# Moving one conditioning piece of a fused two-block kernel from the SSD stage into the attention heads

## The reference, cut to what matters

```
for i in range(2):                                   # DEPTH = 2
    x = x + 0.5 * swiglu(rms_norm(x), ...)           # d_ff 2816
    proj = rms_norm(x) @ w_in[i]
    xbc = silu(causal_depthwise_conv(xbc)) ; y_ssd = ssd_mixer(xbc, dt_raw, z, ...)
    y_att = dilated_attention(q, k, v)               # 16 heads of 64
    x = x + concatenate([y_ssd, y_att]) @ w_out[i]
    x = x + 0.5 * swiglu(rms_norm(x), ...)
...
c_act = silu(c)
mod   = c_act @ w_ada + b_ada                        # 1024 -> 6 * 1024
modf  = c_act @ w_ada_f + b_ada_f                    # 1024 -> 2 * 1024
```

## Time and profile before

| quantity | value |
|---|---|
| median of 3 runs | 2202.26 us (2196.20 to 2210.37) |
| profiled execution, time | 2203.71 us |
| profiled execution, span of the core | 2201.9 us |
| mean granted TensorE clock | 0.978 of full |
| PE busy, share of the span | 96% |
| DVE busy | 75% |
| ACT busy | 50% |
| POOL busy | 21% |

### The profile page before, as it was taken

One profiled execution on the slowest core, in us unless ns is written; L12 is line 12 of the kernel. 1 busy time (PEld: TensorE's weight loads), 2 busy tenths in 40 slices (PEclk: granted clock), 3 DMA queues, 4 the chain that ended last, 5 costly groups with the idle time before them and its releaser, 6 DMA issues. The chain is left out here.

```text
span 2201.9 us, 34859 instructions
## 1 busy us (share of the span) xinstructions
PE 2115.3 (96%) x13433; PEld 1839.4 (84%) x13433; DVE 1655.9 (75%) x2247; ACT 1111.8 (50%) x1291; POOL 455.8 (21%) x239
## 2 busy tenths in 40 slices
PE   6999999999999999999999998999979999999996
PEld 6998999559998998999658997999957777777775
DVE  5665887548666765778538655788789999999998
ACT  4343353334433433354324343524348888888885
POOL 8600180809004500081718100000010000000000
PEclk9999999999998999999999999999989999999999
DMA  8854564436655655464336653435649999999994
GB/s 260 267 183 141 158 213 141 143 125 226 211 176 186 232 184 178 145 200 154 134 134 211 199 193 96 153 116 166 235 155 362 369 369 378 364 362 377 367 366 171
DMA packets 238996, 484.33 MB, mean 220 GB/s; under 512 B 10612, under 2 KB 178848, under 8 KB 222528
## 3 DMA queue, kind: packets, MB, share of 16 engines
q1 hardware_dynamic: 226880, 443.58, 57.5%
q0 software_dynamic: 11424, 37.44, 5.1%
q10 hardware_dynamic: 608, 2.14, 0.2%
HBM read 482.03 MB, written 1.09 MB: 219 GB/s over the span
## 5 line engine op out<-in xcount | busy, mean ns | idle before, releaser
L748 PE MATMUL misc<-xh,ring_low 128*128 128x256 f32 x1536 | 427.9, 279 | 0.0
L747 PE MATMUL misc<-xl,high_b 128*128 128x256 f32 x1408 | 394.0, 280 | 9.4 <-DVE xl L2117 6.9
L749 PE MATMUL misc<-xh,high_b 128*128 128x256 f32 x1408 | 392.0, 278 | 0.0
L748 PEld LDWEIGHTS misc<-xh,ring_low 128*128 128x128 f32 x1536 | 291.9, 190 | 3.4
L2779 DVE TENSOR_TENSOR ring_low<-ring,high_b 128x2048 fp32r<-128x2048 f32 x128 | 287.1, 2284 | 0.0
L747 PEld LDWEIGHTS misc<-xl,high_b 128*128 128x128 f32 x1408 | 267.2, 190 | 13.7 <-DVE xl L2117 7.1
L749 PEld LDWEIGHTS misc<-xh,high_b 128*128 128x128 f32 x1408 | 267.0, 190 | 0.0
L2126 DVE TENSOR_TENSOR ring_low<-ring,high_b 128x2048 fp32r<-128x2048 f32 x88 | 226.2, 2611 | 39.7 <-ACT high_b L1613 39.7
L1890 ACT ACTIVATE high_b<-ring 128x2048 fp32r<-128x2048 f32 x124 | 235.7, 1914 | 33.9 <-DMA ring<-in_w_dram 33.0
L1644 ACT ACTIVATE arena<-arena 128x256 f32<-128x256 f32 x88 | 36.8, 418 | 427.7 <-DVE arena L2160 427.7
L1310 PE MATMUL misc<-high_b,ue 128*128 128x512 f32 x512 | 204.2, 399 | 1.9 <-DVE ue L2822 1.2
(11 more groups left out here) (426 smaller groups left out, 4964.1 us busy)
## 6 DMA issues: line engine op xcount, KB each, us to landing
ring<-in_w_dram SPq DMA_DIRECT2D x128, 1024.0 KB, 7.8
ring<-in_w_in_dram SPq DMA_DIRECT2D x72, 1024.0 KB, 5.5
ring_d<-in_w_dram SPq DMA_DIRECT2D x128, 512.0 KB, 5.2
ring<-in_ffn_w_gate_dram SPq DMA_DIRECT2D x44, 1024.0 KB, 5.4
ring<-in_ffn_w_up_dram SPq DMA_DIRECT2D x44, 1024.0 KB, 7.8
ring_d<-in_ffn_w_down_dram SPq DMA_DIRECT2D x88, 512.0 KB, 7.3
arena<-in_w_ada_dram POOLq DMA_DIRECT2D x48, 512.0 KB, 4.4
ring<-in_w_out_dram SPq DMA_DIRECT2D x20, 1024.0 KB, 4.9
```

What stands on the lines that cost most here:

```text
L747: pe.matmul(dst, wh, ml, start=start, stop=False, **kw)
L748: pe.matmul(dst, wl, mh, start=False, stop=False, **kw)
L749: return pe.matmul(dst, wh, mh, start=False, stop=stop, **kw)
```

## The change

Pool's piece 4l+1 no longer waits for the convolutions of the SSD mixer (`conv_done`) but for the gated SSD rows (`ysd_ready`). PE takes it in the ninth step of the heads (h = 9), between the turned weights of head 7 and the values of head 6; DVE takes it at the end of its step 9. Its fill, M, moves into the list of the attention fills behind T of head 7.

```diff
@@ attention_fills
         if h in TURNS:
             order.append(("Y", TURNS[h]))
+        if h == MOD_AT:
+            order.append("M")
     order.append(("Y", 3))
+MOD_AT = 9
@@ fills
-                  (("v", l, 3), 1), (("qkt", l), 8), (("mod", 4 * l + 1), 1), (("yt", l), 4), (("att", l), 2 * HEADS + 4),
+                  (("v", l, 3), 1), (("qkt", l), 8), (("yt", l), 4), (("att", l), 2 * HEADS + 5),
@@
+    for l in range(DEPTH):
+        FILL.first["mod", 4 * l + 1] = FILL["att", l] + AF["M"]
@@ PE, before the turns of the SSD rows
-                modulation(4 * l + 1)
                 pe.wait_ge(ysd_ready, l + 1)
@@ PE, in the loop over the steps
                         turn_values(TURNS[h])
+                    if h == MOD_AT:
+                        modulation(4 * l + 1)
                     if h >= 3:
                         values(h - 3)
@@ Pool, first block of a piece
                         if p % 4 == 1:
-                            pool.wait_ge(conv_done, NX * (p // 4 + 1))
+                            pool.wait_ge(ysd_ready, p // 4 + 1)
```

## The result

| | before | after |
|---|---|---|
| median | 2202.15 us (8 runs, 2196.20 to 2210.37) | 2221.00 us (8 runs, 2217.04 to 2227.22) |
| ratio | | 1.0081 [1.0062, 1.0099] |
| profiled execution, time and span | 2203.71, 2201.9 us | 2222.78, 2221.0 us |
| mean granted clock | 0.978 | 0.973 |

The change costs 18.9 us, three times the forecast 5.9 and 2 us beyond the upper end of the range. Timed again on another chip, beside the repeats of experiments 3 to 5, it took 2220.36 us (10 runs), 1.0075 [1.0050, 1.0101]. The medians of the experiments and all ratios leave out three slow executions, of 2394 us (experiment 4), 5410 and 6033 us (kernel before).

The account below looks back on a forecast made before the run. PE, busy 96% of the span, was taken to set the time. The terms -3.3 - 0.2 + 3.8 + 0.6 + 1.8 + 1.0 + 2.2 = +5.9 us gave a forecast of 2208 us, range 2197 to 2219.

Parts of the forecast that it names:

- part 1: SSD stage without Pool: PE's gap near 300 us shrinks to 1.0 us; gain 3.3 us in layer 0, 0.2 in layer 1.
- part 2: Eight matmuls moved from ahead of the SSD rows to step 9: +3.8 us, and +0.6 for the clock after the longer standstill.
- Part 3: Bank order: at step 10 scores 11 wait about 0.9 us for line 2422 to free their bank; +1.8 us in all.
- Part 4: Pool beside steps 10 to 18 stretches line 2405, +1.0 us; at the attention's end, a split of line 2126, +2.2 us.
- rival 2: Heads, steps 10 and 11: the clock falls in both layers, +3.4 to +6.8 us, 2215 us at most; chance 0.2.
- One empty step and not two speaks against: Argument against the clock falling at steps 10 and 11: one step there lacks an output unit, not two.
- the spare time: Step 9, layer 0: piece 1 ready at about 439.0, PE asks at 442.2, 3.2 us to spare.
- rival 1: SSD stage: all DVE stretches were on the path, 2193 or 2188 us; milder form 2203; chance together 0.25, strong form 0.05.
- rival 3: Step 9 comes too early for piece 1, PE waits 7.6 us; 12.8 us a layer, 2234 us; chance 0.05.
- rival 4: Nothing moves: layer 0's gap has another reason and the heads hide the rest; 2202 us; chance 0.05.

Follow-up runs that it names:

- Experiment 3: Kernel after, one matmul of 8 columns in place of eight of 1 column for pieces 1 and 5: 2213.25 us, 1.0056; again 2214.13 us.
- experiment 4: Kernel after, the piece's eight columns in unused columns of the bank of scores 9, no fill of their own: 2216.49 us, 1.0069; again 2218.23 us.
- experiment 5: Kernel after, eight columns in scores 9's bank by one matmul: 2202.82, again 2207.93 us; its estimate for the unedited after: work and waiting +12, clock loss +9.
- experiment 2: Kernel after, Pool waits for `conv_done` again, PE and DVE still take the piece at step 9: 2215.72 us, 1.0056.
- experiment 1: Kernel before, Pool's sums and products for pieces 1 and 5 cut to one column, loads and waits kept: 2204.14 us, 1.0008.
- experiment 6: Kernel after, Pool's arithmetic for pieces 2 and 6 cut to one column: 2207.95 us, 1.0019.
- experiment 8: Nothing changed, a second profile of each kernel: before 2200.52 us, after 2202.63 us.
- Experiment 7: Kernel after, Pool's first two loads of pieces 3 and 7 issued only after PE took the piece before: 2220.78 us, 1.0083.

## Why the prediction was wrong

The direction was right, and the time stayed within 1%, which had 0.94 of the chance. The size was not: 13 us are missing from the sum. Of its terms +6.4 us were work and waits and -0.5 us clock (-1.1 in part 1, +0.6 in part 2). The estimate of experiment 5 has some 12 and some 9 us. So two steps of the prediction failed: it counted the new waits too low (parts 3 and 4), and, the larger share, it put what the clock does behind them at nothing and left that to rival 2.

**Part 1: the direction right, the basis a single execution.** The gap at 300 us went from 3.16 to 0.77 us with no low clock behind it, as forecast. But the second look at the kernel before has 1.16 us there and 1.50 in layer 1, where the text had 0.2, and experiment 2, with Pool at work beside the mixer, 1.09 and 1.08. The 3.16 us were mostly the scatter of one profile, and that the forecast gap of 1.0 us came is in part luck; Pool's absence took about 0.3 us from this wait in layer 0 and 0.9 in layer 1 (experiment 2 against after). The mixers are 9.4 us shorter than in the profiled before, and 4.7 shorter than in its second look (187.1 + 184.9), against 3.5 forecast. Some 1.7 us of the 9.4 lie before Pool's piece begins: from 260 to 270 us the granted clock was 0.66 in the profiled before and 0.83 after, and it was 0.66 again in the second timing of the kernel after. In experiment 2 the mixers are short (369.6) with Pool at work beside them, and in experiment 1 they are long (376.2) without its sums. That Pool's arithmetic made the mixers longer is therefore not shown; what did stays open.

**Part 2: the term right, the room behind it not.** The matmuls cost 1.84 us at step 9 and the wait ahead of the SSD rows grew to 4.32 us, where 4.31 was worked out. The turns behind that longer standstill took 3.28 us, not more than before. What was missing is the clock behind a run of matmuls of one column: the unit behind it took 5.00 us in layer 0 and 6.29 in layer 1, and 3.65 in both layers of the quick execution of the same kernel. Experiment 3 takes that away with the columns.

**Part 3 with part 4: the first failing step.** "PE would stand about 0.9 us" came from a step 10 in which line 2405 took 0.17 us, and the stretch of that line stood in another term, at 0.5 us. They are one path. Measured waits: 2.42 (layer 0) and 0.90 (layer 1) at step 10, 2.03 and 1.14 at step 15: 6.5 us where the two terms together had 2.8. With Pool's sums out of the way (experiment 6) the wait at step 10 was 1.25 and 0.89 us, so part 3 by itself was nearly right; what failed was to add Pool's stretch as a small term beside it. By the bounds of the text (1.5 + 1.5 a layer) 6.0 was the end, so the wait alone just leaves them.

**The second failing step: rival 2 was the right mechanism with too low a price and chance.** It gave the falling clock 3.4 us a layer at most, at one place. It fell in four: behind the one-column matmuls, behind the wait at step 10, behind that at step 15, and at the FFN's start. In layer 0 of the profiled execution it came to 6.2 us within the heads, and in the FFN some 28 matmuls stood 0.213 us apart instead of 0.115, another 2.7 us; in experiment 8 the waits were shorter and cost hardly any clock. The argument "One empty step and not two speaks against" read the clock as a matter of a single wait. The Trainium skill's page "TensorE: Matmul & The Clock Gate" (Part 1) says that how many matmuls run at the lower clock differs from run to run of one kernel; the two profiled executions of the kernel after, 20 us apart at the same span times clock, agree.

**Part 4's stretch of line 2126 did not come.** Pool ended piece 2 at 483 and not 490.5, since it had begun at 436.7 and not 444.1, and the splits came later. In its place stood a step that the text called free: "Pool's loads move with the pieces, on a queue of their own; nothing is moved past SP's". The first loads of piece 3 went out as SP asked for the first FFN weights, and the norm turns waited 2.01 and 2.52 us. Experiment 7 shows most of it by removing it, and also that it is worth little in the median. The forecast term (2.2 us) came near the 3.6 us by which these waits grew by luck, since the mechanism was another one.

**Rivals 1, 3 and 4.** Step 9 was not too early: piece 1 had its last sum at 432.9 and PE asked at 434.6. The text had the spare time as 3.2 us; it was 1.7, and in the quick execution of experiment 8 only 0.4, so this rival was avoided narrowly. Rivals 1 and 4 fall with the result.

**What stays open** besides part 1: why taking away the fill and the columns together, or Pool's sums for piece 2 alone, brings most or nearly all of the loss back, while the fill or the columns alone bring 2 to 7 us. The clock could do that, if short standstills close together cost more than the same ones apart, and the clock losses mostly go that way (52 to 53 us after, 48 to 50 with one matmul, 44 to 45 with both edits, 45 with light sums, 44 to 46 before). It was not isolated, and the excess over the plain sum is itself within the noise.

## What to carry to other kernels

In this kernel the stage whose matrix engine has short waits already was a bad host for work of a side engine, even where each wait looked covered. Ask what two small delays do on the same path, and then what the clock does behind them. Look for the stage with the fullest matrix engine and the least to block; here the FFNs took Pool's work for 2.6 us where the heads gave back 8 and the mixers 5 to 9. A moved piece takes along the loads of the piece behind it. And take the waits of a kernel from more than one profile before building a term on one of them: the same gap was 3.16 us in one and 1.16 in the next.

## What the hardware showed that was not expected

- Eight fp32 matmuls of one column, 1.84 us of busy PE, often leave the clock lower behind them: 4.75 to 6.40 us for a unit of 3.65 in 7 of 12 layers profiled with them in step 9, and 4.68 to 5.35 in 4 of 4 with them ahead of scores 9. With one matmul of eight columns (0.39 us) in their place it was 3.65 in 8 of 8.
- A product on 128x2 numbers on DVE, 0.17 us with Pool idle, took 1.35 and 2.17 us and ended within 0.03 us of the Pool sum that ran beside it.
- The kernel after gave 2202.6 us in one execution and up to 2231.3 in others, while the kernel before stayed within 2194.6 and 2210.9 in the counted runs beside all of them.
- Fewer sums on Pool are not less disturbance: the loads of experiment 1 then came in a bunch, and the 70 us around them stayed as slow (66.46 us of PE busy, before 66.84).
